# A hybrid attention and recurrence layer on one core: a mixer's slots in another order, and a state update read as one block

## The chip, the cores and the metric

The kernel runs on one core of a Trainium2 chip. TensorE (PE) does matrix products and transposes into PSUM, VectorE (DVE), ScalarE (ACT) and GpSimd (POOL) do the rest, and SyncE (SP) issues the transfers. Each engine has its own stream of instructions and they meet only through semaphores: an instruction waits until a counter has reached a value, and everything behind it on the same engine waits with it. The metric is the device time of one execution in microseconds (us).

## The reference

One layer works on 256 context tokens and 1024 latent tokens of 1024 channels: normalise and modulate, one input projection, two groups of heads, an output projection, and an MLP. Between the projections stand the two groups that this change touches:

```python
# gated linear attention, 8 heads, forward and backward, chunk by chunk
o = einsum('bhid,bhde->bhie', qc * exp(b), S) + einsum('bhij,bhje->bhie', A, vc)
S = exp(b_last)[..., None] * S + einsum('bhjd,bhje->bhde', kc * exp(b_last - b), vc)

# windowed attention, 8 query heads over 2 key heads, with a sink per head
p = softmax_with_sink(concatenate([s_loc, s_ctx], axis=-1), sink)
o = einsum('...qs,...sd->...qd', p[..., :span], vb) + einsum('...qs,...sd->...qd', p[..., span:], vc)
```

`A` is the masked product of decayed queries and keys of one chunk. The latent tokens see 512 cached context keys and their own block of 128 with its two neighbours.

## The kernel before

The projections, the merge and the MLP stand before and after a function `mixer` (from L1491 on), which computes both groups of heads. The change lies wholly inside it.

**Units and slots.** The windowed attention is cut into 20 units (a tile of 128 tokens times one key head, four query heads each). A latent unit has 6 or 7 blocks of 128 keys, a context unit has 2: 116 blocks in all. A slot takes two blocks, so there are 58 slots, numbered w. In slot w, `scores(g)` (L1810, L1811, L1813 for a masked block) multiplies the keys of blocks 2w and 2w+1 with the queries into the two banks of the tile `st`, ACT's `weights` (L1899) turns them into exponentials `pT`, and `values(g)` (L1828, 32 small products in all) multiplies the weights of the slot before with the values into `pv`. When a unit ends, ACT copies `pv` out (`outputs`, L1905) before the next unit may write it; where a unit ends in the middle of a pair the slot is called late, and its second `values` goes to the slot's end.

**Items ahead.** The softmax needs the largest raw score of each row first. For each later unit these are computed ahead, as items laid on the places (w, 0) and (w, 1) of a slot: two raw products with the 512 context keys (`raw_context`, L1768) or the local ones (`raw_local`, L1778), for which DVE finds the maxima (L1969, L1985, L1990) from the bank pair `score`; and the queries (`queries`, L1760: four transposes, copied by ACT at L1887, their low part made by DVE at L1960) together with the transposed maxima of the unit before (`turn_peaks`, L1784, after DVE's L2001 and before its L2012). A product into `score` must wait until DVE has read what stood in that bank. The lists `ctx_at`, `loc_at`, `query_at` and `turn_at` say which item has which place; a place on which DVE finishes a unit (`finish`, L2023 to L2032) carries none. The lists are not changed.

**The recurrence.** Twenty steps x (ten tiles, two directions) run through the same slots. Steps 0 to 2 stand ahead of slot 0 in a loop of six beats; from then on step x has its scores in the even slot 2(x-3) and its outputs in the odd slot behind it, up to slot 33. `pe_scores` transposes the keys (L1264) for ACT to copy (L1306), and computes the raw scores (L1272), which DVE masks (L1383). `pe_outputs` computes the update of the state (L1285), and then the outputs (L1293, L1297), which ACT copies (L1313). DVE scales the update (L1367, L1394 or L1402), POOL folds it into the state (L1354, L1358), makes the next step's operands (L1347) and scales keys and queries (L1252, L1256). In slots 5 to 47 POOL also works off ten tiles of gated output (L1076 to L1108), with one reduction of each on DVE (L1090) that waits for POOL's L1080; these belong to fixed slots too.

**What sets the order.** Each engine walks the slots in a loop of its own, and what a slot issues, and in which order, is written out there by hand: for PE at L1848 to L1877, for ACT at L1926 on. In PE's slot stand `scores` of the pair, the item of (w, 0), `values`, the item of (w, 1), and then a step's `pe_scores` or `pe_outputs`.

Of the kernel before, what the change touches and what calls it, by code (L numbers as in the profile page):

```python
# [20 lines left out]
P = 128  # L21
# [7 lines left out]
DH = 64  # L29
# [1113 lines left out]
class Recurrence:  # L1143
# [114 lines left out]
    def pe_scores(self, pe, x):  # L1258
        i, d, t = self.place(x)
        pe.wait_ge(self.ke_ready, x + 1)  # L1260
        if x:
            pe.wait_ge(self.new_ready, 2 * x)
        for b in range(self.HP):
            tr = pe.transpose(self.ps[:, 2, b * P:(b + 1) * P], self.ke[:, d, b], self.keep["ident"])  # L1264
        tr.then_inc(self.tr_ready, 1)
        pe.wait_ge(self.qe_ready, x + 1)
        if x:
            pe.wait_ge(self.at_ready, x)
            pe.wait_ge(self.o_kept, x)
        for h in range(H):  # L1270
            rows = slice((h % 2) * DH, (h % 2 + 1) * DH)
            mm = pe.matmul(self.ps[:, h % 2, (h // 2) * P:(h // 2 + 1) * P], self.ke[rows, d, h // 2], self.qe[rows, d, h // 2],  # L1272
                           start=True, stop=True)
        mm.then_inc(self.score_ready, 1)

    def pe_outputs(self, pe, x):
# [5 lines left out]
        for b in range(self.HP):  # L1282
            for half, rows in enumerate(halves):
                c = b * P + half * DH
                mm = pe.matmul(self.ps[rows, 2, c:c + DH], self.kt[:, d, c:c + DH], self.v[:, j, c:c + DH], start=True, stop=True)  # L1285
# [31 lines left out]

    def dve_first(self, dve):
        dve.memset(self.mid[:, 0], 0.0).then_inc(self.zeroed, 1)
        dve.memset(self.decm[:, :, :, :, :], 0.0).then_inc(self.zeroed, 1)  # L1320
        dve.wait_ge(self.zeroed, 2)
        dve.wait_ge(self.dec_ready, 1)
# [9 lines left out]
    def wait_state(self, eng, x):  # L1332

        if x < 2:
            eng.wait_ge(self.new_ready, 2 * x + 2)
        else:
            eng.wait_ge(self.state_ready, x - 1)
# [12 lines left out]
    def pool_state(self, pool, x):  # L1350
        i, d, t = self.place(x)
        st = self.state[0 if i < NTP else 1]
        self.wait_state(pool, x - 1)
        pool.tensor_tensor(self.kept[:, :, :], st[:, d], self.decayed(d, t, slice(0, P), 1), ALU.mult).then_inc(self.kept_ready, 1)  # L1354
        pool.wait_ge(self.new_ready, 2 * x + 2)
        pool.wait_ge(self.kept_ready, x - 1)
        pool.wait_ge(self.mid_ready, 2 * x - 2)
        pool.tensor_tensor(st[:, d], self.kept[:, :, :], self.new[:, :, :], ALU.add).then_inc(self.state_ready, 1)  # L1358

    def dve_new(self, dve, x):  # L1360
        i, d, t = self.place(x)
        dve.wait_ge(self.ds_ready, x + 1)
        self.wait_state(dve, x - 1)
        for half in range(2):
            rows = slice(half * DH, (half + 1) * DH)
            upd = self.ps[rows, 2].rearrange("p (b c) -> p b c", c=P)[:, :, half * DH:(half + 1) * DH]
            dve.tensor_tensor(self.new[rows], upd, self.decayed(d, t, rows, 2), ALU.mult).then_inc(self.new_ready, 1)  # L1367
# [18 lines left out]
    def dve_state(self, dve, x):  # L1386
        i, d, t = self.place(x)
        st = self.state[0 if i < NTP else 1]
        if i == 0:
            dve.wait_ge(self.ds_ready, x + 1)  # L1390
            for half in range(2):
                rows = slice(half * DH, (half + 1) * DH)
                upd = self.ps[rows, 2].rearrange("p (b c) -> p b c", c=P)[:, :, half * DH:(half + 1) * DH]
                dve.tensor_tensor(st[rows, d], upd, self.decayed(d, t, rows, 2), ALU.mult).then_inc(self.new_ready, 1)  # L1394
# [4 lines left out]
        for half in range(2):  # L1399
            rows = slice(half * DH, (half + 1) * DH)  # L1400
            upd = self.ps[rows, 2].rearrange("p (b c) -> p b c", c=P)[:, :, half * DH:(half + 1) * DH]
            dve.tensor_tensor(self.new[rows], upd, self.decayed(d, t, rows, 2), ALU.mult).then_inc(self.new_ready, 1)  # L1402
        dve.wait_ge(self.new_ready, 2 * x + 2)
# [87 lines left out]
def mixer(nc, keep, a, scratch, outs, s2, raw, keys, ahead, rec, prj_stored, mod_out):  # L1491
# [20 lines left out]
    with ExitStack() as ctx:  # L1512
# [129 lines left out]
        with nc.Block() as block:  # L1642
# [105 lines left out]
            def _(pe):  # L1748
# [85 lines left out]
                for k in range(BEATS + 1):  # L1834
                    if k < BEATS:
                        if k % 2 == 0:
                            rec.pe_scores(pe, k // 2)
# [10 lines left out]
                for w in range(SLOTS + 2):  # L1848
                    if w == 0:
                        pe.wait_ge(tables, 5)  # L1850
                        pe.wait_ge(filled, 3)
                        keys.pe_ones(pe)
                    if w < SLOTS:
                        scores(2 * w)
                        scores(2 * w + 1)
                    ahead((w, 0))
                    late = 1 <= w <= SLOTS and crossing(w)
                    if 1 <= w <= SLOTS:
# [3 lines left out]
                    if w == 0:  # L1862
                        rec.pe_scores(pe, scores_at[w])
                    ahead((w, 1))
                    if w and w in scores_at:
# [5 lines left out]
                    if w == SLOTS - 1:  # L1871
                        pe.wait_ge(rec.at_ready, X)
                        pe.wait_ge(rec.new_ready, 2 * X)
# [8 lines left out]
            def _(act):  # L1882
# [43 lines left out]
                for w in range(SLOTS + 2):  # L1926
                    if w < SLOTS:
                        weights(2 * w)
                        weights(2 * w + 1)
                    if (w, 0) in query_at:  # L1930
                        high_queries(query_at[w, 0])
# [3 lines left out]
                    if (w, 1) in query_at:  # L1935
                        high_queries(query_at[w, 1])
                    if w in scores_at:
                        rec.act_turned(act, scores_at[w])
# [1264 lines left out]
```

## Time and profile before

| | |
|---|---|
| median of 3 runs | 1687.52 us (1684.58 to 1689.86) |
| the profiled execution, its own time | 1684.21 us |
| its span | 1682.3 us |
| PE busy | 1603.9 us, 95% |
| DVE, POOL, ACT busy | 1020.3, 1016.3, 673.6 us |

The span begins with the first instruction of the profile and ends with the last. Slot 0 starts at 415.2 us (first L1810) and the last `values` ends near 697 us, so the slots take some 281 us of the 1682. The rest are the projection before and the merge and MLP behind, which the change does not touch. A PE that counts as busy need not run at its peak: a product of 512 columns has a duration of 0.39 us or more in the rows, while the next one may start 0.23 us after it. What PE loses is therefore read from starts, not from the busy share.

### The profile page before, as it was taken

How to read it: one execution, taken by the hardware profiler on the slowest of the kernel's cores; microseconds unless marked ns; L12 is line 12 of the kernel's file. 1: busy time of each engine (PE TensorE's matmuls, PEld its weight loads, DVE VectorE, ACT ScalarE, POOL GpSimd, SP SyncE). 2: the span in 40 equal slices, each digit the busy share in tenths (PEclk: the TensorE clock that was granted, in tenths of full speed). 3: DMA queues.
4: the chain of work that ended last, by engine and by line, in shares of the span. 5: the costliest groups of instructions: out<-in, count | busy, mean ns of one | idle time of the engine just before them, and what ended most of it. 6: DMA issues, size and time to landing. Idle time of an engine off the chain costs nothing.

```text
span 1682.3 us, 31906 instructions
## 1 busy us (share of the span) xinstructions
PE 1603.9 (95%) x11618; PEld 1394.7 (83%) x11618; DVE 1020.3 (61%) x1584; ACT 673.6 (40%) x1192; POOL 1016.3 (60%) x758
## 2 busy tenths in 40 slices
PE   4999999998999888899999999999999999999997
PEld 1998778996777766788888998989978899998996
DVE  2713565666676669455866566575695545545468
ACT  2514224225444345312354444444535444444441
POOL 1711554654574789002487787777898667667682
PEclk9999999999999999999999999999999999999999
DMA  9254565659555455333661322313235132231322
GB/s 331 92 159 137 196 210 175 224 179 263 160 171 158 158 158 152 108 130 142 200 224 57 100 75 75 100 51 99 88 114 174 51 100 72 78 100 50 99 64 100
DMA packets 211450, 225.93 MB, mean 134 GB/s; under 512 B 52752, under 2 KB 171664, under 8 KB 208144
## 3 DMA queue, kind: packets, MB, share of 16 engines
q1 hardware_dynamic: 209248, 224.46, 41.6%
q8 instruction: 70, 1.15, 0.3%
q10 hardware_dynamic: 2096, 0.02, 0.1%
q14 instruction: 36, 0.29, 0.1%
HBM read 177.22 MB, written 47.24 MB: 133 GB/s over the span
## 4 chain that ended last, share of the span: by engine, by line
PE 43%; POOL 4%; DVE 2%; issue 1%; ACT 0%; DMA 0%; SPq 0%; DVEq 0%; ACTq 0%; POOLq 0%
PE ff_banks L3095 8%; PE ff_banks L3096 8%; PE ff_banks L3097 8%; PE ff_banks L3068 7%; PE ff_banks L3070 7%; PE ff_banks L3069 7%; POOL h_whi L2734 1%; POOL h_xop L2332 1%; POOL h_wlo L2746 1%; POOL h_whi L2741 1%; DVE ff_tmp L2935 1%; DVE ff_acc L2925 0%; DMA ff_hb<-in_w_ff 0%; DVE ff_acc L2919 0%; DVE ff_acc L2892 0%
## 5 line engine op out<-in xcount | busy, mean ns | idle before, releaser
L3068 PE MATMUL ff_banks<-h_xop,h_whi 128*128 128x320 f32 x888 | 275.2, 310 | 5.8 <-DVE wo_raw L2872 3.1
L3070 PE MATMUL ff_banks<-h_xop,h_whi 128*128 128x320 f32 x888 | 274.4, 309 | 0.0
L3069 PE MATMUL ff_banks<-h_xop,h_whi 128*128 128x320 f32 x888 | 274.4, 309 | 0.0
L2892 DVE TENSOR_TENSOR ff_acc<-ff_acc,ff_banks 128x512 f32<-128x512 f32 x294 | 199.0, 681 | 99.2 <-PE ff_banks L3097 99.2
L3095 PE MATMUL ff_banks<-h_wlo 128*128 128x512 f32 x600 | 234.3, 390 | 1.6 <-DVE ff_acc L2892 0.8
L3097 PE MATMUL ff_banks<-h_wlo 128*128 128x512 f32 x600 | 233.5, 389 | 0.0
L2734 POOL TENSOR_TENSOR h_whi<-mid_raw,h_whi 128x512 fp32r<-128x512 f32 x149 | 207.2, 1406 | 1.4 <-ACT h_whi L2586 1.4
L2746 POOL TENSOR_TENSOR h_wlo<-mid_raw,h_wlo 128x320 fp32r<-128x320 f32 x128 | 116.6, 913 | 129.6 <-ACT mid_raw L2623 129.6
L3068 PEld LDWEIGHTS ff_banks<-h_xop,h_whi 128*128 128x128 f32 x888 | 166.7, 188 | 9.5 <-issue 4.8
L3069 PEld LDWEIGHTS ff_banks<-h_xop,h_whi 128*128 128x128 f32 x888 | 166.7, 188 | 1.1
L3070 PEld LDWEIGHTS ff_banks<-h_xop,h_whi 128*128 128x128 f32 x888 | 166.7, 188 | 0.0
L972 PE MATMUL prj_banks<-prj_whi,h_hi 128*128 128x304 f32 x480 | 147.8, 308 | 3.3 <-DVE h_lo L341 2.2
L2734 POOL TENSOR_TENSOR h_whi<-ff_tmp,h_whi 128x512 fp32r<-128x512 f32 x63 | 105.5, 1674 | 67.7 <-ACT h_whi L2586 67.7
L974 PE MATMUL prj_banks<-prj_whi,h_lo 128*128 128x304 f32 x480 | 145.2, 303 | 0.0
L973 PE MATMUL prj_banks<-prj_wlo,h_hi 128*128 128x304 f32 x480 | 144.7, 301 | 0.0
L3095 PEld LDWEIGHTS ff_banks<-h_wlo 128*128 128x128 f32 x600 | 112.6, 188 | 25.8 <-DVE ff_acc L2892 1.9
L3096 PE MATMUL ff_banks<-h_whi,h_wlo 128*128 128x512 f32 x340 | 132.4, 389 | 0.0
L3097 PEld LDWEIGHTS ff_banks<-h_wlo 128*128 128x128 f32 x600 | 112.6, 188 | 23.6
L2586 ACT ACTIVATE h_whi<-mid_raw 128x512 fp32r<-128x512 f32 x149 | 89.9, 622 | 97.7 <-DVE mid_raw L2848 91.4
L2616 ACT ACTIVATE mid_raw<-wo_raw 128x320 f32<-128x320 f32 x128 | 60.3, 471 | 160.0 <-DVE wo_raw L2870 66.4
L3096 PE MATMUL ff_banks<-h_wlo 128*128 128x512 f32 x300 | 117.0, 390 | 0.0
L825 ACT ACTIVATE prj_stage<-prj_banks 128x304 f32<-128x304 f32 (+2 forms) x47 | 21.0, 446 | 220.7 <-PE prj_banks L974 133.9
(306 smaller groups left out, 3774.2 us busy)
## 6 DMA issues: line engine op xcount, KB each, us to landing
mid_raw<-in_w_ff SPq DMA_DIRECT2D x124, 512.0 KB, 4.3
mid_raw<-in_w_ada SPq DMA_DIRECT2D x18, 1024.0 KB, 7.2
early_room<-qk_by_channel SPq DMA_DIRECT2D x20, 512.0 KB, 4.1
proj<-prj_stage SPq DMA_DIRECT2D x60, 152.0 KB, 1.9
mid_raw<-in_w_in SPq DMA_DIRECT2D x6, 1216.0 KB, 7.2
early_room<-in_w_ada SPq DMA_DIRECT2D x6, 1024.0 KB, 10.9
decays<-early_room SPq DMA_DIRECT2D x8, 640.0 KB, 4.5
early_room<-decays SPq DMA_DIRECT2D x20, 256.0 KB, 2.9
```

The source lines that it names most:

```text
L972: pe.matmul(out, x_hi, whi[j][:, k, 0:w], start=(k == 0), stop=False)
L973: pe.matmul(out, x_hi, wlo[j][:, k, 0:w], start=False, stop=False)
L974: mm = pe.matmul(out, x_lo, whi[j][:, k, 0:w], start=False, stop=(k == KD - 1))
L2734: pool.tensor_tensor(lo, source(q, i), hi.bitcast(F32), ALU.subtract).then_inc(w1lo_ready, 1)
L2746: pool.tensor_tensor(ulo[j][c][:, t0:t0 + TH], v[i % 2], uhi[j][c][:, t0:t0 + TH].bitcast(F32), ALU.subtract).then_inc(ulo_ready, 1)
L2892: dve.tensor_tensor(acc[:, p, at], acc[:, p, at], down[n % RING], ALU.add).then_inc(added, 1)
L3068: pe.matmul(out, w_hi[:, k], x_hi[:, k], start=(k == 0), stop=False)
L3069: pe.matmul(out, w_hi[:, k], x_lo[:, k], start=False, stop=False)
L3070: mm = pe.matmul(out, w_lo[:, k], x_hi[:, k], start=False, stop=(k == KH - 1))
L3095: pe.matmul(out, x_hi, w_hi[c][:, at], start=(c == 0), stop=False)
L3096: pe.matmul(out, x_hi, w_lo[c][:, at], start=False, stop=False)
L3097: mm = pe.matmul(out, x_lo, w_hi[c][:, at], start=False, stop=(c == 1))
```

## The change

It has two parts.

1. **The order in a slot.** On PE the item of (w, 0) goes first, then the two `scores`, then the key transposes of a recurrence step (a function of its own now, `pe_turned`), then the item of (w, 1), then the step's score products, then `values` and, in odd slots, the outputs. In a late slot the step's scores stay behind the first `values`. ACT follows: its query copy for (w, 0) goes ahead of the two `weights`, and its copy of the turned keys goes ahead of the query copy for (w, 1) and of the end of a unit. The order on DVE, POOL and SP stays.
2. **The state update.** The products of both heads of a pair are written to the same 64 columns, one head to the upper and one to the lower half of the partitions. Where DVE had two operations, each 64 partitions by 256, it has one of 128 by 256, and the counter `new_ready` counts steps and not halves.

```diff
-                mm = pe.matmul(self.ps[rows, 2, c:c + DH], self.kt[:, d, c:c + DH], self.v[:, j, c:c + DH], start=True, stop=True)
+                mm = pe.matmul(self.ps[rows, 2, b * DH:(b + 1) * DH], self.kt[:, d, c:c + DH], self.v[:, j, c:c + DH], start=True, stop=True)
...
+    def update(self):
+        return self.ps[:, 2, 0:self.HP * DH].rearrange("p (b c) -> p b c", c=DH)
...
-        for half in range(2):
-            rows = slice(half * DH, (half + 1) * DH)
-            upd = self.ps[rows, 2].rearrange("p (b c) -> p b c", c=P)[:, :, half * DH:(half + 1) * DH]
-            dve.tensor_tensor(self.new[rows], upd, self.decayed(d, t, rows, 2), ALU.mult).then_inc(self.new_ready, 1)
+        dve.tensor_tensor(self.new[:, :, :], self.update(), self.decayed(d, t, slice(0, P), 2), ALU.mult).then_inc(self.new_ready, 1)
...
+                    ahead((w, 0))
                     if w < SLOTS:
                         scores(2 * w)
                         scores(2 * w + 1)
-                    ahead((w, 0))
+                    if w in scores_at:
+                        rec.pe_turned(pe, scores_at[w])
+                    ahead((w, 1))
                     late = 1 <= w <= SLOTS and crossing(w)
+                    if w in scores_at and not late:
+                        rec.pe_scores(pe, scores_at[w])
                     if 1 <= w <= SLOTS:
                         values(2 * w - 2)
                         if not late:
                             values(2 * w - 1)
-                    if w == 0:
-                        rec.pe_scores(pe, scores_at[w])
-                    ahead((w, 1))
-                    if w and w in scores_at:
+                    if w in scores_at and late:
                         rec.pe_scores(pe, scores_at[w])
...
                 for w in range(SLOTS + 2):
+                    if (w, 0) in query_at:
+                        high_queries(query_at[w, 0])
                     if w < SLOTS:
                         weights(2 * w)
                         weights(2 * w + 1)
-                    if (w, 0) in query_at:
-                        high_queries(query_at[w, 0])
+                    if w in scores_at:
+                        rec.act_turned(act, scores_at[w])
+                    if (w, 1) in query_at:
+                        high_queries(query_at[w, 1])
                     for u in ending(w):
                         outputs(u)
                         sink_term(u)
-                    if (w, 1) in query_at:
-                        high_queries(query_at[w, 1])
-                    if w in scores_at:
-                        rec.act_turned(act, scores_at[w])
```

The lines of `mixer` stand at most three lower or higher in the changed file (L1828 is L1825 there, L1810 is L1807). On PE, the even slot 6 before: scores, a raw local item, values, a raw context item, the recurrence.

```order
L1810 MATMUL mix_st<-mix_qdup,mix_khl 128x512
L1811 MATMUL mix_st<-mix_qlow,mix_kone 128x512
L1810 MATMUL mix_st<-mix_qdup,mix_khl 128x512
L1811 MATMUL mix_st<-mix_qlow,mix_kone 128x512
L1778 MATMUL mix_score<-mix_khl,mix_qdup 128x384 x2
L1828 MATMUL mix_pv<-mix_vx,mix_pT 64x65 x16
L1768 MATMUL mix_score<-mix_khl,mix_qdup 128x512 x2
L1264 MATMUL mix_gla<-keep_mats,early_ke 128x128 x4
L1272 MATMUL mix_gla<-early_qe,early_ke 128x128 x8
```

The same slot 6 on PE in the changed kernel.

```order
L1775 MATMUL mix_score<-mix_khl,mix_qdup 128x384 x2
L1807 MATMUL mix_st<-mix_qdup,mix_khl 128x512
L1808 MATMUL mix_st<-mix_qlow,mix_kone 128x512
L1807 MATMUL mix_st<-mix_qdup,mix_khl 128x512
L1808 MATMUL mix_st<-mix_qlow,mix_kone 128x512
L1264 MATMUL mix_gla<-keep_mats,early_ke 128x128 x4
L1765 MATMUL mix_score<-mix_khl,mix_qdup 128x512 x2
L1275 MATMUL mix_gla<-early_qe,early_ke 128x128 x8
L1825 MATMUL mix_pv<-mix_vx,mix_pT 64x65 x16
```

Between the two raw items stood `values`; now the scores and the key transposes stand there. The recurrence scores and `values` are neighbours at the slot's end.

The odd slot 3 on PE before, up to the first of its output products.

```order
L1810 MATMUL mix_st<-mix_qdup,mix_khl 128x512
L1811 MATMUL mix_st<-mix_qlow,mix_kone 128x512
L1810 MATMUL mix_st<-mix_qdup,mix_khl 128x512
L1811 MATMUL mix_st<-mix_qlow,mix_kone 128x512
L1778 MATMUL mix_score<-mix_khl,mix_qdup 128x384 x2
L1828 MATMUL mix_pv<-mix_vx,mix_pT 64x65 x16
L1768 MATMUL mix_score<-mix_khl,mix_qdup 128x512 x2
L1285 MATMUL mix_gla<-early_room,early_kt 64x64 x8
L1293 MATMUL mix_gla<-early_mid,early_qe 64x128 x2
```

And slot 3 in the changed kernel.

```order
L1775 MATMUL mix_score<-mix_khl,mix_qdup 128x384 x2
L1807 MATMUL mix_st<-mix_qdup,mix_khl 128x512
L1808 MATMUL mix_st<-mix_qlow,mix_kone 128x512
L1807 MATMUL mix_st<-mix_qdup,mix_khl 128x512
L1808 MATMUL mix_st<-mix_qlow,mix_kone 128x512
L1765 MATMUL mix_score<-mix_khl,mix_qdup 128x512 x2
L1825 MATMUL mix_pv<-mix_vx,mix_pT 64x65 x16
L1288 MATMUL mix_gla<-early_room,early_kt 64x64 x8
L1296 MATMUL mix_gla<-early_mid,early_qe 64x128 x2
```

Here only the four score products part the two raw items, and `values` stands next to the state update and the outputs.

## Rows read from the trace of the kernel before

**Rows 1.** Windows over the slots: duration, then busy time of each engine, clock, DMA.

```profile
640.00:670.00 30.00, 25.29 (x352) 19.10 (x353) 27.43 (x45) 16.26 (x30) 27.70 (x23) 1.00 0.59 177
...
sum 281.00, PE 257.15 PEld 200.36 DVE 196.41 ACT 129.96 POOL 189.10; mean PE 25.72 PEld 20.04 DVE 19.64 ACT 13.00 POOL 18.91
```

**Rows 2.** Waits of PE from 390 to 700 us: total, times, longest.

```profile
PE mix_score L1768 <- DVE mix_qlow L1960: 7.6, 8, 2.5
...
PE mix_score L1778 <- DVE mix_topc L1969: 4.0, 4, 2.8
PE mix_score L1778 <- DVE mix_qlow L1960: 3.6, 4, 1.7
...
PE mix_score L1784 <- DVE mix_peak L2001: 1.6, 3, 0.6
```

**Rows 3.** Timeline of PE, slot 3: start, duration, instruction.

```profile
431.91 0.51 PE L1810 MATMUL mix_st<-mix_qdup,mix_khl 128*128 128x512 f32 x1
432.25 0.40 PE L1811 MATMUL mix_st<-mix_qlow,mix_kone 100*128 100x512 f32 x1
432.49 0.40 PE L1810 MATMUL mix_st<-mix_qdup,mix_khl 128*128 128x512 f32 x1
...
432.96 0.51 PE L1778 MATMUL mix_score<-mix_khl,mix_qdup 128*128 128x384 f32 x2
433.40 1.15 PE L1828 MATMUL mix_pv<-mix_vx,mix_pT 128*64 128x65 f32 x32
434.49 1.00 PE L1768 MATMUL mix_score<-mix_khl,mix_qdup 128*128 128x512 f32 x2
```

**Rows 4.** Timeline of all engines, slot 16: turned peaks, recurrence scores, DVE's mask.

```profile
509.12 0.32 PE L1784 MATMUL mix_score<-keep_mats,mix_peak 128*100 128x128 f32 x1 [0.51 <-DVE mix_peak L2001]
509.28 0.60 PE L1264 MATMUL mix_gla<-keep_mats,early_ke 128*128 128x128 f32 x4
...
509.81 1.16 PE L1272 MATMUL mix_gla<-early_qe,early_ke 64*128 64x128 f32 x16
...
511.09 1.22 DVE L1383 TENSOR_TENSOR early_at<-mix_gla,keep_mats 128x1024 f32<-128x1024 f32 x1
```

**Rows 5.** Timeline of slot 5: from the queries' transposes to the next raw item.

```profile
443.43 0.60 PE L1760 MATMUL mix_score<-keep_mats,mix_xq 128*128 128x128 f32 x4
...
444.12 0.59 ACT L1887 ACTIVATE mix_qdup<-mix_score 128x512 fp32r<-128x512 f32 x1
444.75 0.68 DVE L1960 TENSOR_TENSOR mix_qlow<-mix_score,mix_qdup 64x512 fp32r<-64x512 f32 x1 [1.09 <-ACT mix_qdup L1887]
445.46 0.70 DVE L2012 TENSOR_TENSOR mix_qlow<-mix_score,mix_negd 4x512 fp32r<-4x512 f32 x1
445.58 0.47 PE L1768 MATMUL mix_score<-mix_khl,mix_qdup 128*128 128x512 f32 x1 [0.36 <-DVE mix_qlow L1960]
```

**Rows 6.** Timeline of DVE ahead of slot 0: whole and half operations.

```profile
414.44 0.83 DVE L1397 TENSOR_TENSOR mix_kept<-mix_state_p,keep_dec 128x256 f32<-128x256 f32 x1
415.30 0.88 DVE L1402 TENSOR_TENSOR mix_new<-mix_gla,keep_dec 64x256 f32<-64x256 f32 x2
```

**Rows 7.** Timeline of PE in the beats.

```profile
408.19 1.08 PE L1264 MATMUL mix_gla<-keep_mats,early_ke 128*128 128x128 f32 x4 [3.33 <-DVE mix_state_p L1394]
```

**Rows 8.** The window behind that wait.

```profile
409.00:415.00 6.00, 6.00 (x83) 5.22 (x83) 5.60 (x13) 2.23 (x4) 1.29 (x2) 0.65 0.90 306
```

**Rows 9.** Timeline of all engines, slots 28 and 29.

```profile
582.09 0.69 DVE L1090 TENSOR_REDUCE mix_glo_ssq<-mid_raw 128x8 f32<-128x512 f32 x1 [2.32 <-POOL mid_raw L1080]
582.69 1.28 DVE L1969 TENSOR_REDUCE mix_topc<-mix_score 128x1 f32<-128x512 f32 x2
...
583.52 0.41 PE L1778 MATMUL mix_score<-mix_khl,mix_qdup 128*128 128x384 f32 x1 [2.77 <-DVE mix_topc L1969]
```

**Rows 10.** Timeline of PE, the late slot 45, which has no item at (45, 1).

```profile
658.01 0.69 PE L1828 MATMUL mix_pv<-mix_vx,mix_pT 128*64 128x65 f32 x16
659.87 0.69 PE L1828 MATMUL mix_pv<-mix_vx,mix_pT 128*64 128x65 f32 x16 [1.17 <-ACT mix_sums L1905]
```

More of the change, by code:

```diff
@@ L1256, in pool_scaled, with pe_turned @@
         pool.tensor_tensor(self.qe[:, d], self.up[:, d], self.qk[:, j, 0:self.HP], ALU.mult).then_inc(self.qe_ready, 1)
-    def pe_scores(self, pe, x):
+    def pe_turned(self, pe, x):
         i, d, t = self.place(x)
@@ L1261, in pe_scores @@
         if x:
-            pe.wait_ge(self.new_ready, 2 * x)
+            pe.wait_ge(self.new_ready, x)
         for b in range(self.HP):
@@ L1265, in pe_scores @@
         tr.then_inc(self.tr_ready, 1)
+    def pe_scores(self, pe, x):
+        i, d, t = self.place(x)
         pe.wait_ge(self.qe_ready, x + 1)
@@ L1334, in wait_state @@
         if x < 2:
-            eng.wait_ge(self.new_ready, 2 * x + 2)
+            eng.wait_ge(self.new_ready, x + 1)
         else:
@@ L1354, in pool_state @@
         pool.tensor_tensor(self.kept[:, :, :], st[:, d], self.decayed(d, t, slice(0, P), 1), ALU.mult).then_inc(self.kept_ready, 1)
-        pool.wait_ge(self.new_ready, 2 * x + 2)
+        pool.wait_ge(self.new_ready, x + 1)
         pool.wait_ge(self.kept_ready, x - 1)
@@ L1390, in dve_state @@
             dve.wait_ge(self.ds_ready, x + 1)
[L1391 to L1394, printed above, removed]
+            dve.tensor_tensor(st[:, d], self.update(), self.decayed(d, t, slice(0, P), 2), ALU.mult).then_inc(self.new_ready, 1)
             return
@@ L1398, in dve_state @@
         dve.wait_ge(self.ds_ready, x + 1)
[L1399 to L1403, printed above, removed]
+        dve.tensor_tensor(self.new[:, :, :], self.update(), self.decayed(d, t, slice(0, P), 2), ALU.mult).then_inc(self.new_ready, 1)
+        dve.wait_ge(self.new_ready, x + 1)
         dve.wait_ge(self.kept_ready, x - 1)
@@ L1836, in _ @@
                         if k % 2 == 0:
+                            rec.pe_turned(pe, k // 2)
                             rec.pe_scores(pe, k // 2)
@@ L1872, in _ @@
                         pe.wait_ge(rec.at_ready, X)
-                        pe.wait_ge(rec.new_ready, 2 * X)
+                        pe.wait_ge(rec.new_ready, X)
                         early.pe_turn(pe, mT, keep["ident"])
```

## The prediction

> **What bounds the kernel now.** I read the busy shares of the page first (in the table above: PE 95% of the span), then the windows over the 58 slots, then PE's waits there, and last the timeline of single slots. The change touches only the slots, about 281 us of the 1682. In them PE counts as busy for 257.15 us, DVE for 196.41 and POOL for 189.10 [rows 1]: PE is the bound, but not everywhere. From 640 to 670 us DVE is busy for 27.43 and POOL for 27.70 of 30 us [rows 1]; there PE could not go much faster whatever its order. What PE still loses is of two kinds. One is waits: four sorts stand in [rows 2], 7.6, 4.0, 3.6 and 1.6 us, all of them raw items (or turned peaks) that wait for DVE, 16.8 us together. The other shows in no wait. In slot 3 the second product of the scores starts 0.34 us after the first (431.91, 432.25), the next one 0.24 us later (432.49) [rows 3]. The first stood behind small products of another shape. The same loss stands on the way back: two raw products of 384 columns take 0.44 us to the start of `values` (432.96, 433.40), where by their columns (three quarters of 512, so 0.18 us each) they should take 0.35 [rows 3]. So each step between full 128 x 128 products and products on half of the array costs PE some 0.10 us.
>
> **Term 1: fewer such steps.** I class each group by its tile as the rows write it: 128\*128 (scores, raw items, transposes), 64\*128 (recurrence scores) and 128\*64 (`values`, state update, outputs) [rows 3, 4]. An even slot went full, `values`, full, recurrence scores, full: four steps. Now it goes full, recurrence scores, `values`, full: three. An odd slot went full, `values`, full, outputs, full: four. Now `values` and outputs are neighbours: two. Going through all slots with the lists of items, the late slots included, I count 185 steps before and 133 after; 50 of the 52 fall in slots 0 to 33. Behind slot 33 there is one excursion per slot either way. 50 x 0.10 us = 5.0 us less. Bounds: the 17 places where `values` now touches the state update have no row before; were they to cost as much as a step, 33 x 0.09 = 3.0 us, and at the dearest row (0.34 less 0.23) 50 x 0.11 = 5.5 us.
> The Trainium skill ("TensorEngine Tiling (Array Packing)", Key Properties) says that changing the tiling mode, and not merely the tile, drains TensorE. By that rule the 17 new neighbours, both 128\*64, cost nothing, and the term stays 5.0; if instead every change of operands cost 0.10 us, it would be 3.3. No row here has `values` beside the state update.
>
> **Term 2: the first wait.** In the beats PE waits 3.33 us for DVE's L1394, the two halves of a state update [rows 7]. Two halves take 0.88 us; a whole operation of 128 x 256 took 0.83 in the same place [rows 6], though one of its halves shows 0.44, and what I expect is that the duration goes by the 256 elements of a row. So 0.05 to 0.44 us less; I take 0.4. The 17 later merges (slots 1 to 33) free DVE 0.44 us each, but in odd slots, behind `values`, where nothing on PE waits for DVE soon: nothing. Behind the 3.33 us the granted clock was 0.65 from 409 to 415 us [rows 8], so part of it at the lower of its levels (1.2 against 2.4 GHz). A wait of 2.9 is long still, and I expect that stretch to stay slow. Were it to stay at the high level, some 2 us would go as well (6 us of which 0.35 of the cycles were missing: 2.1).
>
> **Term 3: even slots have more cover.** Between two raw items stood `values`, 1.09 us (433.40 to 434.49) [rows 3]. In an even slot there now stand four score products (0.93) and the key transposes (0.53, 509.28 to 509.81 [rows 4]): 1.46 us. Where a raw local item and then the queries with the turned peaks stand in an even slot (10, 16, 22), PE waited for the peaks: 0.51 us of idle at 509.12 [rows 4], 1.6 us in all three [rows 2]. An idle begins only when the last product has drained, so each wait costs a little more than its idle; I take 0.6 us each, 1.8 us less. A pair of raw products whose second has to wait shows it by its length: at 434.49 it takes 1.00 us, where two products 0.23 us apart would take some 0.63 [rows 3]. That one is in an odd slot; four even slots show the same 0.3 to 0.4 us, and with 0.37 more cover I take 1.2 us less. The queries at (w, 0) of slots 2, 8 and 28 take 2.15 us from PE's transposes to the raw item that needs them (443.43 to 445.58), and the second of the pair needs DVE's L2012, to 446.16 [rows 5]. ACT now copies them ahead of the weights. But in an even slot ACT comes out of the outputs and decays of the odd slot before, so I take only 0.5 us for the three. Sum 3.5 us, bounds 1 to 5.
>
> **Term 4: odd slots have less.** There only the score products part the two raw items: 0.93 us for 1.09, with a mask 1.17. And DVE comes late to them. Counted from the first raw item of an even slot: second raw item at 1.9 us, recurrence scores done at 3.6, DVE's mask (1.22 us [rows 4]) from 3.9 to 5.1, its pair of maxima for the odd slot's first item (1.28 us [rows 9]) from 5.3 to 6.6, first half done at 5.95. PE reaches the odd slot's first item at 4.7 and the second at 6.2: the first of that pair goes, the second needs 6.6 and would be there at 6.4. So 0.25 us of new wait without a mask, none with one, and 0.6 where the mask of an earlier peak or a query copy comes between. Eleven odd slots have two items; with what they waited before (some 1.6 us) I take 2.4 us more. Bounds 0 and 11 x 0.9 = 10 us.
>
> **Term 5: what POOL sets.** In slot 28 DVE sat 2.32 us at L1090 until POOL's L1080 was done, and PE then 2.77 us [rows 9]. POOL works off its tile of gated output in a chain of its own, and DVE's reduction stands in a fixed slot. What PE gains between slots 24 and 28 is waited for here: 1 us given back. Behind it, up to slot 47, PE gains nothing more by term 1, and DVE and POOL leave no room [rows 1].
>
> **Term 6: late slots without recurrence.** In slot 45 the second `values` waits 1.17 us for ACT's copy, with no item between [rows 10]. Slot 38 had a raw item there, which now stands ahead: 0.7 us more.
>
> New waits elsewhere: the key transposes wait for DVE's scaled update earlier in the slot than before. It is done about 1.5 us after the update products, and the outputs, an item and four score products (some 3.7 us) come first: nothing. Behind it on PE would stand a raw item and the recurrence scores. ACT's query copy ahead of the weights delays those by 0.6 us, and their readers are a slot away: nothing. PE's scores need the weights of the slot before, with `values` in between: nothing.
>
> **The sum.** -5.0 - 0.4 - 3.5 + 2.4 + 1.0 + 0.7 = -4.8 us. Against the profiled execution (1684.2, with the span 1682.3): 1679.4. That execution is 3.3 us below the median of the runs shown, so as a median 1687.5 - 4.8 = **1682.7 us**. A measurement of this kernel tells about 0.3%, 5.1 us, from no change, and my forecast lies just inside.
>
> **The rivals.**
> - *More waits go than I take.* If the 16.8 us of [rows 2] shrink by half (8.4) beside terms 1 and 2, with 1.7 given back by terms 5 and 6: -12, 1675.5. For it: ACT's copy comes first, and DVE is 0.44 us freer in odd slots. Against: most of these waits are a chain of ACT and DVE that starts on PE, and PE arrives at its end as early as before.
> - *DVE takes up the gain.* Even and odd slot together, DVE sets the pace: the steps between shapes are saved and waited for. 0.2 us more in each of the 17 pairs of slots is 3.4 us: -1.4, 1686.1. For it: the mask and two pairs of maxima stand in a row in term 4, and PE is ahead of DVE by 0.2 us only.
> - *Slower: the odd slots' second item.* Place: the raw item at (w, 1) of the eleven odd slots with two items, behind DVE's mask. Price: the whole pair of maxima exposed, 1.28 us each, 14 us, less the 5.0 + 0.4 + 3.5 of gains and plus 1.7: +7, 1694.5. It decides from about 0.66 us of added wait per slot (7.2 us of gain left over eleven slots). Against: it needs DVE to be 1 us later than my count.
> - *That the change doesn't do what it says*, for PE: the order shows that it does; only the merge could be worth nothing, which is 0.4 us and lies in the forecast.
>
> **How the numbers follow.** Forecast 0.50, more waits gone 0.15, DVE takes it up 0.22, slower 0.13. The forecast's own range by its bounds is 1678 to 1688; just under half of it (0.27) lies beyond 5.1 us. Faster: 0.27 + 0.15 = 0.42. Slower 0.13. Same: 0.23 + 0.22 = 0.45. The range, 1676 to 1692, leaves out half of the first rival and most of the last.
>
> **What would show it.** Step 1 right: in the profile after, the first score product behind a raw item is followed 0.23 us later by the second, and L1825 to L1288 takes 1.08 us as L1828 did. Wrong if that last is 1.18. Term 2: PE's wait at L1264 in the beats is 2.9 us. Term 3: no wait for the peaks in slots 10, 16, 22. Term 4: new waits of PE for L1969 or L1985 in odd slots, 0.2 to 0.6 us each; if they are over 0.7, the slower case is here; if there are none, the first rival. Term 5: a longer wait of DVE at L1090 in slot 28. All of it would be wrong if another stage than 390 to 697 us changed its length.

## The result: slower, and where the time went

The changed kernel takes 1695.74 us (median of four runs, 1693.93 to 1698.32) beside 1686.59 for the kernel before: ratio 1.0054, interval 1.0032 to 1.0075. Measured once more beside other kernels (below) it gave 1.0033, interval 1.0019 to 1.0046. So it is slower, by 5.6 us in one measurement and 9.1 in the other. The forecast was 1682.7.

The granted clock and the start of the first slots differ from one execution to the next, so I read the two profiled executions stage by stage, from PE's first score product of a slot to that of another:

| stage | before | after |
|---|---|---|
| end of the projection to slot 0 | 27.78 | 30.54 |
| slots 0 to 33 | 196.12 | 191.35 |
| slots 34 to 57 (the tail), to the transposes of L2128 | 84.06 | 95.91 |
| from L2128 to the end | 986.9 | 986.3 |

The first line is noisy by itself: 27.5 to 31.0 us in all profiles of this study. ACT waits there 4.3 to 7.5 us for a load of decays; how much of the spread comes from that is not shown. In the new order the item of (w, 0) stands ahead of a slot's first score product, so both boundaries of the head lie 0.5 to 0.6 us later in the work of their slot. Slots 0 to 33 (the head) became 4.8 us shorter, about what terms 1 to 5 say (5.5). The 24 slots behind them, to which the prediction gave 0.7 us in all, became 11.9 us longer. A second profile of the changed kernel has 192.0 and 96.1 us for the two.

PE's waits in the changed kernel from 390 to 710 us (total, times, longest); they answer to [rows 2]:

```profile
PE mix_score L1765 <- DVE mix_qlow L1960: 9.9, 9, 2.8
PE mix_score L1775 <- DVE mix_qlow L1960: 5.5, 4, 1.7
PE mix_score L1757 <- DVE mix_topl L1985: 4.9, 3, 2.4
PE mix_gla L1264 <- DVE mix_state_p L1394: 3.8, 2, 3.3
PE mix_score L1781 <- DVE mix_peak L2001: 3.4, 5, 1.3
...
PE mix_score L1775 <- DVE mix_topc L1969: 1.9, 4, 0.9
```

The waits for `topc` halved (4.0 to 1.9). Those for `topl` in front of the queries grew from 1.1 to 4.9, and those for `qlow`, the copied queries, from 11.2 to 15.4.

Slot 47 of the changed kernel shows one kind of new wait, on all engines (some rows between are left out):

```profile
670.35 0.66 PE L1757 MATMUL mix_score<-keep_mats,mix_xq 128*128 128x128 f32 x4
...
670.87 0.48 PE L1807 MATMUL mix_st<-mix_qdup,mix_khl 128*128 128x512 f32 x1
...
671.90 0.39 PE L1810 MATMUL mix_st<-mix_maskb,mix_identb 128*128 128x512 bf16 x1
672.39 0.60 ACT L1887 ACTIVATE mix_qdup<-mix_score 128x512 fp32r<-128x512 f32 x1 [1.90 <-PE mix_st L1810]
...
673.02 0.68 DVE L1960 TENSOR_TENSOR mix_qlow<-mix_score,mix_qdup 64x512 fp32r<-64x512 f32 x1 [2.83 <-ACT mix_qdup L1887]
...
673.85 0.36 PE L1775 MATMUL mix_score<-mix_khl,mix_qdup 128*128 128x256 f32 x1 [1.55 <-DVE mix_qlow L1960]
```

ACT has been idle for 1.90 us, the queries have been transposed since 671.0, and yet the copy L1887 is released by `mix_st`: by the last score product of its own slot. It starts at 672.39, when PE has nothing left but the raw item that needs the copy. The same slot of the kernel before, PE and ACT:

```profile
664.18 0.60 PE L1760 MATMUL mix_score<-keep_mats,mix_xq 128*128 128x128 f32 x4
...
664.83 1.15 PE L1828 MATMUL mix_pv<-mix_vx,mix_pT 128*64 128x65 f32 x32
664.88 0.59 ACT L1887 ACTIVATE mix_qdup<-mix_score 128x512 fp32r<-128x512 f32 x1
666.50 0.35 PE L1778 MATMUL mix_score<-mix_khl,mix_qdup 128*128 128x256 f32 x1 [0.52 <-DVE mix_qlow L1960]
```

There the copy followed the transposes by 0.7 us, beside `values`. The cause stands in two lines that the change did not touch. Copies of queries lie in a ring of four (`QRING`), and L1886 lets unit u's copy start only when the last scores of unit u - 4 are done: `act.wait_ge(st_ready, begin[u - QRING + 1])`. The planner (`while ... at[0] < done_slot[u + 1 - QRING] - 1`) puts the queries as early as that allows, in the very slot that holds those last scores. That cost nothing while the scores stood at the head of the slot. Now (w, 0) stands there. In slots 40, 47 and 53 PE's wait for the copied queries was 0.32, 0.52 and 0.37 us and is now 1.55 in each. Not every wait of this kind is new: slots 44 and 50 had 1.02 and 1.68 us and have 0.70 and 1.72.

The second kind is at the head of slot 44, PE and DVE:

```profile
649.67 2.33 DVE L1140 TENSOR_TENSOR h_wlo<-wo_raw,h_whi 128x1024 fp32r<-128x1024 f32 x1 [1.50 <-ACT h_whi L1132]
651.93 1.23 DVE L2023 TENSOR_TENSOR mix_den<-mix_sums,mix_sb_out 128x4 f32<-128x4 f32 x1
...
653.40 1.13 DVE L2032 TENSOR_TENSOR mix_mixa<-mix_sums,mix_inv 128x256 f32<-128x256 f32 x1
...
654.46 0.47 DVE L1985 CUSTOM_DVE_ANT_0 mix_junk<-mix_score,mix_maskr,mix_topc 128x256 f32<-128x256 f32 x1
```

```profile
651.91 1.15 PE L1825 MATMUL mix_pv<-mix_vx,mix_pT 128*64 128x65 f32 x32
655.09 0.63 PE L1757 MATMUL mix_score<-keep_mats,mix_xq 128*128 128x128 f32 x4 [2.02 <-DVE mix_topl L1985]
656.85 0.45 PE L1781 MATMUL mix_score<-keep_mats,mix_peak 128*100 128x128 f32 x1 [1.13 <-DVE mix_peak L2001]
...
660.16 1.22 PE L1775 MATMUL mix_score<-mix_khl,mix_qdup 128*128 128x256 f32 x2 [0.70 <-DVE mix_qlow L1960]
```

DVE works in order through a step of the output weights, the end of a unit and the maxima; PE stands for 2.02 us with the scores of two blocks, which need nothing from it, queued behind the wait. Before, they were issued first and covered it. Slot 40 has the same wait, 2.40 us (1.11 before). The size varies: in the second profile of the same kernel slot 40 has 2.39, slot 44 only 1.08, and there DVE's L1140 took 1.23 us for 2.33.

The third is what follows from both. The windows 636 to 648 and 656 to 668 us (duration, busy time of PE, PEld, DVE, ACT, POOL, then the clock), in the kernel before and then in the changed one:

```profile
636.00:648.00 12.00, 9.33 (x110) 6.53 (x108) 11.47 (x22) 6.29 (x12) 10.46 (x9) 1.00 0.62 177
656.00:668.00 12.00, 9.75 (x124) 7.40 (x125) 10.51 (x16) 6.86 (x12) 11.47 (x10) 1.00 0.62 197
```

```profile
636.00:648.00 12.00, 10.01 (x83) 6.83 (x82) 7.70 (x16) 3.60 (x6) 5.93 (x5) 0.58 0.45 131
656.00:668.00 12.00, 9.79 (x79) 6.83 (x79) 7.23 (x12) 4.98 (x9) 9.33 (x8) 0.57 0.80 245
```

PE is as busy in both, but does 83 and 79 instructions where it did 110 and 124: for most of these stretches the granted clock is the lower of its two levels, 1.2 GHz. `values`, 1.15 us at the high level, takes 2.00 there.

Over the whole tail PE's waits add up to 12.1 us before and to 18.0 and 16.5 in the two profiles of the changed kernel. The time at the lower level is 3.4 us before and 20.5 and 23.8 after, an estimate from the clock of windows of 4 us. So longer waits are 4 to 6 of the 12 us, and the rest goes with PE working at the lower level behind them; that is a reading, which the filled waits below test only in part.

### The profile page after: what moved, and what is told of

The parts are those of the page before. It is cut to its first block and busy times, and to the rows that moved or that the text cites. A ratio compares the mean times of both kernels' runs of the same rounds, so it can differ in the third digit from the quotient of the medians.

```text
span 1692.1 us, 31886 instructions
## 1 busy us (share of the span) xinstructions
PE 1604.2 (95%) x11618; PEld 1397.3 (83%) x11618; DVE 1020.0 (60%) x1564; ACT 671.8 (40%) x1192; POOL 1014.5 (60%) x758
## 3 DMA queue, kind: packets, MB, share of 16 engines
q8 instruction: 70, 1.15, 0.3%
```

## Experiments

The names in the expectations: theory A is that the loss lies in the order of the slots behind 33 (and in slot 26), where waits for DVE have lost the scores as cover; theory R that it is the ring of query copies; theory W that it is the output weights in DVE's queue. Rival B is the merged update, C the clock by chance, D the beats. All were measured beside the kernel before; 0.001 of the ratio is 1.7 us. The expectations give absolute times for a kernel before of 1686.6 us; beside these kernels it took 1686.75 to 1688.99, on four chips, so the ratio decides. Kernels in groups of one chip can be compared by their times too: the first two, the one with three slots and the one with three filled waits; even, tail alone, seven query slots and one more buffer; odd, changed again, queries later and even filled; the four with the weights late.

| kernel | ratio | interval | us against before |
|---|---|---|---|
| update merged, order of before | 0.9997 | 0.9987 to 1.0007 | -0.5 |
| new order in slots 0 to 33 only | 0.9975 | 0.9965 to 0.9986 | -4.2 |
| even ones of them only | 0.9970 | 0.9959 to 0.9981 | -5.1 |
| odd ones of them only | 1.0018 | 1.0006 to 1.0030 | +3.0 |
| slots 34 to 57 only | 1.0070 | 1.0048 to 1.0091 | +11.8 |
| changed kernel, again | 1.0033 | 1.0019 to 1.0046 | +5.6 |
| order of before in slots 26, 40, 44 | 1.0010 | 1.0001 to 1.0019 | +1.7 |
| order of before in seven query slots | 1.0020 | 1.0008 to 1.0032 | +3.4 |
| one more buffer in the ring | 1.0013 | 0.9998 to 1.0029 | +2.2 |
| queries one slot later | 1.0006 | 0.9994 to 1.0018 | +1.0 |
| weights late, order of before | 0.9996 | 0.9982 to 1.0010 | -0.7 |
| weights late, changed kernel | 1.0021 | 1.0008 to 1.0035 | +3.5 |
| weights late and one more buffer | 0.9991 | 0.9977 to 1.0005 | -1.5 |
| weights late, even slots only | 0.9960 | 0.9945 to 0.9975 | -6.8 |
| three waits filled with products | 1.0022 | 1.0010 to 1.0033 | +3.7 |
| even slots, first wait filled | 0.9967 | 0.9950 to 0.9983 | -5.6 |

**Which slots.** The edit puts the order of before under a condition on the slot, on PE and in the same way on ACT; it alone differs between these kernels (`True`, `w >= 34`, `w >= 34 or w % 2`, `w >= 34 or w % 2 == 0`, `w < 34`):

```diff
+                    if w >= 34:
+                        if w < SLOTS:
+                            scores(2 * w)
+                            scores(2 * w + 1)
+                        ahead((w, 0))
...
+                        ahead((w, 1))
...
+                    else:
                         ahead((w, 0))
```

PE's and ACT's order move together in all of these kernels; what ACT's alone is worth is not known.

> The order of the slots as before, the state update in one operation instead of two halves. Theory A (the loss is in the order of slots 34 to 57 and 26): the merged update is worth what it was forecast, 0.4 us at the first wait; 1685.5 to 1687.5 where the kernel before has 1686.6, and PE's wait at L1264 in the beats is 2.9 to 3.3 us. Rival B (the merged update is what costs, by the later start of slot 0 at 418.5 against 415.2 us): 1690 or more.

> The new order in slots 0 to 33, the order of before on PE and ACT in slots 34 to 57, the merged update. Theory A: the forecast gains of slots 0 to 33 stay (PE was 6.7 us nearer from slot 0 to slot 39) and the 13.8 us that slots 40 to 57 lost are gone: 1680 to 1685, faster than before by 2 to 6 us. Rival C (the lower clock stretches come by chance, and the order is worth nothing): 1686 to 1691. Rival D (the beats and the late decays cost 3 us and stay): within 1684 to 1688.

> The new order in the even slots of 0 to 33 alone. By the terms of the prediction the even slots save 17 steps between shapes (1.7 us) and 3.5 us of cover, the odd ones 33 steps (3.3 us) less 2.4 us of new waits: 1682 to 1684 by the terms. If the gain of the head is the steps alone, the even slots give only 1.7 us of it: 1685 to 1687.

> The new order in the odd slots of 0 to 33 alone. The even ones alone gave 5.0 us, both together 4.2 us less than before. By the prediction's terms the odd slots save 3.3 us of steps and lose 2.4 us of cover: 1685.5 to 1687. If the new waits eat more than the steps (the mechanism of the prediction's slower case), 1688 to 1692.

> The new order in slots 34 to 57 alone, the order of before in slots 0 to 33, the merged update. If head and tail add up (changed kernel +9.1, head alone -4.2 by the ratio 0.9975), the tail alone costs 13 us: 1699 to 1702. If the tail only loses because PE arrives there early from the head and finds DVE behind, the tail alone costs less than 8 us: 1690 to 1695.

The merged update is worth nothing that can be measured, for or against: rival B is out. The gain of the first 34 slots (-4.2) and the loss of the last 24 (+11.8) add up to +7.6, within what the changed kernel shows: rivals C and D are out too, since the order alone moves the time both ways and the beats are the same in the first two kernels. The loss is not DVE being caught up with by an early PE, for it is there in full without the head's gain (the tail of that profile takes 96.9 us). Within the head all of the gain is the even slots'; the odd ones alone cost 3.0, which is the outcome that the expectation had for waits that eat more than the steps. There PE waits from 410 to 620 us, in the kernel with odd slots only:

```profile
PE mix_score L1775 <- DVE mix_topc L2000: 5.4, 7, 3.4
...
PE mix_score L1765 <- DVE mix_topl L2016: 2.7, 7, 0.9
```

The wait of 3.4 us is in slot 29, which had 2.77 before. In part the rest is the mixture: behind the second raw item of an even slot of before come the key transposes and the recurrence scores, and an odd slot of the new order begins with its raw item, without the four score products that stood ahead of it before. How large that part is was not measured. The next two kernels have a stronger form of it.

**Which of the late slots.** The same condition, `w in (26, 40, 44)` and `w in (34, 37, 40, 44, 47, 50, 53)`.

> The changed kernel with the order of before in slots 26, 40 and 44 alone. These are the three slots in which, in the changed kernel, PE waits 2.80, 2.40 and 2.02 us at the head of the slot for DVE. Theory A in its narrow form (it is these three places): 1683 to 1687, so 9 to 12 us below the changed kernel. Theory A in its wide form (the whole tail is worse, each slot a little): 1689 to 1693. If nothing comes back (1694 to 1697) the places named are not the cause.

> The order of before in the seven slots behind 33 that have queries (34, 37, 40, 44, 47, 50, 53) and nowhere else. Theory R and theory A both say that these are the places: 1681 to 1686, as with the order of before in all slots behind 33 (1682.8). If the loss is spread over the tail: 1686 to 1690.

Both missed the narrow form of theory A. The first, 1689.69, is where its wide form lies: three slots give back some 4 to 7 us, not 9 to 12. The second gave no more back for seven slots (the two intervals overlap), where 1681 to 1686 was expected. Behind each such slot without a recurrence step the raw item of (w, 1) and that of the next slot's head are neighbours on PE, and there waits of 0.2 to 0.7 us for `topc` and `topl` came up. Mixed orders understate what the places cost; they do show that three slots matter.

**The ring.** One more buffer, in columns of the output weights not yet written then; the units behind 14 shift by one, and only unit 19 keeps its wait. In the second kernel no buffer is added, but the planner's rule is moved by one slot:

```diff
+        def qhi(u):
+            return whi[:, 0:HG, D - P:D] if u == 14 else qdup[:, (u if u < 14 else 10 if u == 19 else u - 5) % QRING]
...
+        def ring_free(eng, u):
+            if u >= QRING and u != 14:
+                eng.wait_ge(st_ready, begin[u - QRING + 1] if u in (19, *range(14)) else begin[u - 4])
```

```diff
-                while u + 1 >= QRING and at[0] < done_slot[u + 1 - QRING] - 1:
+                while u + 1 >= QRING and at[0] < done_slot[u + 1 - QRING]:
```

> The changed kernel with one more buffer in the ring of query copies for the units 14 to 18, so that ACT's copy L1887 in slots 37, 40, 44, 47 and 50 no longer waits for the scores of its own slot (slot 53 still does); order and all else as changed. Theory R (the loss behind slot 34 comes from the ring: the copy may start only when the last scores of the unit four before are done, and these now stand behind the queries): in the changed kernel the copy in slot 47 started at 672.39, 1.0 us after the transposes allow, and PE then waited 1.55 us; without it about 0.3. Slots 40, 44, 47 and 50 give back 1.55 + 0.7 + 1.25 + 1.25 = 4.8 us, and up to 5 us more if the granted clock stays high: 1686 to 1691. Theory A (only the cover in front of PE's waits for the maxima is gone, the ring does not matter): 1694 to 1696.

> The changed kernel with the planner's rule for the queries' place one slot later (the copy's buffer must have been read by the end of the slot before): the queries of slots 37, 40, 44, 47, 50, 53 move to 38, 41, 45, 48, 51, 54. Theory R: the copies no longer wait for their own slot's scores, and the time is that of the kernel with one more buffer, 1686 to 1690. What speaks against: everything behind the queries (raw items, maxima, peaks) has one slot less until the unit's own scores need it; if that decides, 1691 to 1695. Theory A (the ring does not matter): 1694 to 1697.

The first comes out where theory R says. The second, 1691.12, lies above its 1686 to 1690; by the ratio it is 1687.6 for a kernel before of 1686.6, which lies inside. Slot 47 with the extra buffer (L1768 are the transposes, L1897 is the copy, L1786 the raw item):

```profile
662.43 0.66 PE L1768 MATMUL mix_score<-keep_mats,mix_xq 128*128 128x128 f32 x4
...
663.12 0.60 ACT L1897 ACTIVATE mix_qdup<-mix_score 128x512 fp32r<-128x512 f32 x1 [0.55 <-PE mix_score L1768]
...
664.99 0.35 PE L1786 MATMUL mix_score<-mix_khl,mix_qdup 128*128 128x256 f32 x1 [0.62 <-DVE mix_qlow L1970]
```

The copy is released by the transposes now, and PE's wait falls from 1.55 to 0.62. The tail takes 88.8 us in this profile and 89.6 in the other, against 95.9. Beside the changed kernel on the same chip (1695.68), the moved rule gave 1691.12: 4.6 us, with intervals of the ratios that just part (1.0019 and 1.0018).

One wait did not go: in slot 50 the copy now starts behind the transposes, at 672.38, and PE still waits 1.72 us. DVE holds it up, with a weights step and the end of a unit (L1140, L2032 to L2041) ahead of the low part of the queries (L1970):

```profile
672.38 0.60 ACT L1897 ACTIVATE mix_qdup<-mix_score 128x512 fp32r<-128x512 f32 x1 [0.41 <-PE mix_score L1768]
674.50 0.68 DVE L1970 TENSOR_TENSOR mix_qlow<-mix_score,mix_qdup 64x512 fp32r<-64x512 f32 x1
675.32 0.35 PE L1786 MATMUL mix_score<-mix_khl,mix_qdup 128*128 128x256 f32 x1 [1.72 <-DVE mix_qlow L1970]
```

**The weights in DVE's queue.** Six of the eight steps go to later slots, in four kernels:

```diff
-        wo_at = dict(zip((37, 38, 40, 41, 44, 45, 48, 50), range(D // P)))
+        wo_at = dict(zip((37, 38, 46, 48, 50, 51, 53, 55), range(D // P)))
```

> The kernel before, with six of the eight steps of the output weights (DVE's L1140, 1.2 to 2.3 us each) moved from slots 40, 41, 44, 45, 48, 50 to 46, 48, 50, 51, 53, 55. Control for the three others: with the order of before PE waits 1.11 us at the queries of slot 40 and none at those of 44, so 0 to 2 us less: 1685 to 1688. If it gains 4 us or more, the weights' place is a loss of its own and says nothing on the order.

> The changed kernel with the same move of the output weights. Theory W (what the ring leaves of the tail's loss is PE at the head of slots 40 and 44 behind DVE, whose queue holds a weights step there): the waits of 2.40 and 2.02 us for topl shrink below 1 us, and 3 to 5 us go: 1689 to 1692, with the ring's waits in 47, 50 and 53 still there. If the waits stay, DVE is late for another reason (the finish of a unit, L2023 and L2032): 1693 to 1696.

> The changed kernel with one more buffer for the query copies and the output weights late. Theories R and W together: ring 4.4 to 7 us and weights 3 to 5 us less than the changed kernel: 1683 to 1687, the tail (slot 34 to its end) at 84 to 86 us as in the kernel before (84.06) against 95.9. If 1688 or more, something else in the tail's order costs.

> The fastest so far (the new order in the even slots of 0 to 33 alone, ratio 0.9970) with the output weights late. Its tail has the order of before, so by theory W 0 to 2 us less: 1680 to 1682.5 beside a kernel before of 1687.5.

With the order of before the move is worth nothing (0.9996). In the changed kernel the wait at the head of slot 44 is gone; that of slot 40 is not (2.40), since the steps of slots 37 and 38 and the end of a unit are still ahead of it. So theory W holds for one of its two places, and the time does not settle what that is worth: 1.0021 against 1.0033, with intervals that overlap. With the extra buffer too the kernel is level with the kernel before, 1685.47, and between those two kernels of one chip the ring is worth 4.7 us again (their intervals do not meet). But the tail's loss is not gone: its tail takes 88.2 us, where 84 to 86 was expected and the two kernels with the weights late and a tail of before have 81.9 and 81.6. What brings the total level is the head. One of its waits the move of the weights made itself: in slot 47 PE waits 1.60 us, since a weights step stands ahead of the low part of the queries now. The last is the lowest time of the study, 1681.56 beside 1687.69: it beats both kernels of the case, though not clearly the even slots alone (0.9960 and 0.9970, overlapping).

**The clock.** Products whose results nobody reads are put where PE stood idle:

```diff
+                    if w in (26, 40, 44):
+                        pe.wait_ge(p_ready, 2 * w - 1)
+                        for _ in range(10):
+                            pe.matmul(st[:, 0], khl[:, 0, 0:P], khl[:, 0, 0:HALF], start=True, stop=True)
                     ahead((w, 0))
```

> The changed kernel with ten added products of 512 columns (10 x 0.23 = 2.3 us of PE) at the head of slots 26, 40 and 44, whose results nobody reads; they lie where PE waited 2.80, 2.40 and 2.02 us. The waits for DVE stay, so by waits alone the time is the changed kernel's or up to 1 us more: 1695 to 1697. If the price is the granted clock that falls behind a long wait (37.5 us at the lower level against 13.65 before), PE keeps the high level there: 16 to 27 us fewer at the lower level, and the time falls by 5 to 12 us to 1684 to 1690.

> The new order in the even slots of 0 to 33 alone (1681.7), and twelve products of 512 columns in front of the key transposes of the third recurrence step, where PE otherwise stands idle for 2.9 us; nobody reads their results. If the granted clock falls because of that idle time (8 us at the lower level behind it), it stays high and 2 to 4 us go: 1678 to 1680. If the late decays set the start of slot 0 anyway (ACT waits 6.3 to 7.5 us for them), or the clock falls all the same: 1681 to 1683.

The first gave 1.0022, 2 us less than the second measurement of the changed kernel and 5 less than the first, with added work; the intervals overlap, so its size is not settled. The clock rose in part: 0.86 and 0.72 in the two windows above, for 0.58 and 0.57. Over the tail, 10.2 us at the lower level are left of 20.5 to 23.8, and the tail takes 93.9 us for 96, with 4.6 us of added products in it. So the clock's own price is not cleanly measured. In the second the same was done in the beats, with the even slots' kernel:

```profile
408.05 2.91 PE L1838 MATMUL mix_gla<-mix_khl 128*128 128x512 f32 x12
411.09 0.63 PE L1264 MATMUL mix_gla<-keep_mats,early_ke 128*128 128x128 f32 x4
...
412.75 0.65 PE L1757 MATMUL mix_score<-keep_mats,mix_xq 128*128 128x128 f32 x4
...
415.63 0.78 PE L1288 MATMUL mix_gla<-early_room,early_kt 128*64 128x64 f32 x16 [1.75 <-ACT early_kt L1309]
416.14 0.71 PE L1296 MATMUL mix_gla<-early_mid,early_qe 128*64 128x128 f32 x4
```

The four transposes of queries took 0.65 us where they took 1.11 in both kernels of the case. Then PE waited 1.75 us for ACT, which had waited for the decays, and the clock fell behind that. The time did not change (0.9967 against 0.9970). The rows of the other kernels mostly fit the reading that long stretches at the lower level stand behind waits close to each other: with the extra buffer, slot 40 still has its wait of 2.31 us but not the one of 1.55 behind it, and the window 636 to 648 has clock 1.00; with the weights late, slot 40 has both and 0.57, slot 44 no longer its 2.02 us, and the window 656 to 668 has 1.00. A single wait was not free of it either: in the kernel before, the one of 2.51 us in slot 37 has some 3.4 us at the lower level behind it.

## Why the prediction was wrong

**The part that held.** Term 1: the step between shapes. Where `values` stands beside another shape it still takes 1.08 us; beside the state update it takes less than I said (slot 5 of the changed kernel, PE):

```profile
447.31 1.15 PE L1825 MATMUL mix_pv<-mix_vx,mix_pT 128*64 128x65 f32 x32
448.29 0.64 PE L1288 MATMUL mix_gla<-early_room,early_kt 128*64 128x64 f32 x16
```

0.98 us to the update; 1.08 was my sign of being right, a value that still has the 0.10 us in it. So neighbours of one shape save the 0.10 us, as counted, and the first score product behind a raw item is followed by the second 0.23 us later. The Trainium skill ("TensorEngine Tiling (Array Packing)", Key Properties) says that a change of the tiling mode drains TensorE, and not merely a change of the tile. The trace agrees with it: `values` and the update, both 128\*64, show no step. Term 3: even slots alone gave 5.1 us, where their 17 steps (1.7) and term 3 (3.5) say 5.2. With an interval of 3.2 to 6.9 us, so close a match is luck, and the two parts were not measured apart. Of the waits for peaks, those of slots 16 and 22 went; slot 10 keeps 0.39.

**Terms that were off without deciding.** Term 2: one operation for two halves takes 0.42 us for 0.88, as said. PE's wait in the beats was 3.31 us in the first profile of the changed kernel and 2.88, as forecast, in the second and in the kernel with the update alone. Yet that last kernel's ratio is 0.9997: nothing measurable came of it. Term 4: odd slots were to lose 2.4 us against 3.3 of steps, so gain 0.9; beside the even ones they added 0.9 +- 2.6 us to the time, alone they cost 3.0. That is the slower rival's mechanism at a fraction of its price. A place that term 4 did not name is odd slot 13, where PE waits 1.31 us for the peaks (1.28 in the second profile) and had no wait before. Term 5: its sign did not come; DVE, which waited 2.32 us for L1080 in slot 28, waits there no longer. Term 6: 0.58 us in slot 38, but slot 45's 1.17 became 0.58 as well: nothing.

**The step that failed.** "Behind it, up to slot 47, PE gains nothing more by term 1, and DVE and POOL leave no room." I took a saturated DVE as a reason why nothing could change there, and costed slots 34 to 57 at 0.7 us (term 6). They cost 11.8, alone. A full queue means that PE will wait for it; what a wait costs depends on what PE has issued before it, and the change took the scores and `values` from in front of exactly these waits. And I wrote of the query copy ahead of the weights that it "delays those by 0.6 us, and their readers are a slot away: nothing". I followed the copy forward, to its readers, and not backward, to what it waits for: L1886 hangs it on the scores that the change had just put behind it. What the runs show of the tail's 11.8 us: the ring is worth 4.6 and 4.7 us in two pairs of kernels of one chip each, where the three waits themselves grew by 3.4. DVE's queue in front of the maxima is seen in slots 40 and 44; moving the weights removed the wait of slot 44, and its worth, some 2 us by the ratios, is inside the noise. The remainder, about half, stays open: the kernel with both mended still has a tail 6.3 to 6.7 us longer than its like in the order of before (one profile each). The head of slot 40, the ring's share in unit 19 and the lower clock behind these waits are in it and were not told apart. The slower rival was put in the odd slots of the head, where the new order was argued in detail, and not where the plan is different. That its 1694.5 us lies close to the measured 1695.7 is a coincidence.

## What to carry over

When an item moves ahead of another, read its waits, and read also which rule placed it: a planner's "as early as allowed" holds for one order only, and every buffer ring that it counts on is a wait at zero slack. Cost each phase of a pipeline by itself: a phase whose other engine is full is where a lost cover costs most, not least. And check a new order per phase (here even slots early, the old order late), since the sum of a gain and a loss is what the whole change shows.

## What the runs showed of the hardware

DVE's three operations of 128 x 4 elements with two inputs in each unit (L2001, L2005, L2023) mostly take 0.14 to 0.18 us, and now and then 1.2. In the 18 profiles there are 1080 of them; 387 take more than 0.25 us, and every one of these ends within 0.06 us of the end of an operation of POOL that had started before it. L2023 at 651.93 above, and in the changed kernel further, DVE and then POOL:

```profile
655.62 1.18 DVE L2001 TENSOR_TENSOR mix_peak<-mix_topl,mix_sink 128x4 fp32r<-128x4 f32 x1
```

```profile
650.89 2.25 POOL L1076 TENSOR_TENSOR mix_glo_o<-mid_raw 128x512 f32<-128x512 f32 x1
655.51 1.26 POOL L1084 TENSOR_TENSOR mix_glo_si<-mid_raw,mix_glo_factor 128x512 f32<-128x512 f32 x1
```

651.93 + 1.23 is 653.16 and 650.89 + 2.25 is 653.14; 655.62 + 1.18 is 656.80 and 655.51 + 1.26 is 656.77. So on the path of the maxima a tiny operation cost up to 1 us more by what POOL happened to do. All four have two inputs in SBUF. The Trainium skill ("SBUF — State Buffer", SBUF: two separate sides) says that a DVE operation with two SBUF inputs and a GpSimd operation share a pair of ports as an exclusive lock, held for the whole instruction; these ends agree with it. Some short ones did run while a POOL operation was under way, most of them beside its `rstd` of 128 x 8 elements, so not every overlap costs. It was seen, not tested.
